# Ranking the experts on chip: 21 places of 64 rows, with down weights in runs of 8 KB

## The reference, cut to what matters

```python
grp = argmax(softmax(h @ w_group + b_group))            # 4 groups
lg = (h @ w_router + b_router)[:, grp]                  # the 8 experts of that group
p_in, e_in = top_k(softmax(lg), 2)                      # two experts of 32 for each token
...
xb = the tokens of each expert, in order of expert, padded
y = (silu(xb @ w_gate[e]) * (xb @ w_up[e])) @ w_down[e] # 1024 -> 512 -> 1024
out = sum of a token's two rows of y, each by its weight
```

## Time and profile before

| | |
|---|---|
| three executions | 2873.58, 2877.64, 2879.01 us, median 2877.64 |
| the profiled execution | 2871.41 us, span of its instructions 2869.6 us |
| granted TensorE clock, mean over the span | 0.993 |
| busy | TensorE (PE) 97%, VectorE (DVE) 39%, ScalarE (ACT) 27%, GpSimd (POOL) 8% |
| HBM | 582.7 MB read, 52.0 MB written, 221 GB/s over the span |
| DMA queue of SyncE | 519.68 MB, 46.9% of 16 engines' span |
| DMA queue of GpSimd | 115.07 MB, 11.7% |

### The profile page before, as it was taken

How to read it: one execution, slowest core, us unless ns; L and a number is a source line. 1 busy time by engine, 2 the same in 40 slices (tenths; PEclk the granted TensorE clock), 3 DMA queues, 4 the chain that set the end, 5 groups by cost and what they waited for, 6 DMA issues and landing times. The chain is left out here.

```text
span 2869.6 us, 64937 instructions
## 1 busy us (share of the span) xinstructions
PE 2778.4 (97%) x27105; PEld 1646.9 (57%) x27109; DVE 1117.6 (39%) x2687; ACT 761.2 (27%) x1601; POOL 234.2 (8%) x396
## 2 busy tenths in 40 slices
PE   7999999999989999999999999989999999999998
PEld 4544655444644467546666666634675566666664
DVE  2582643672643255463222222273443522222224
ACT  1211521102642167421111111153774111111111
POOL 3000011000020000011000000020000100000001
PEclk9999999999999999999999999999999999999999
DMA  7212843123734000347999999872003699999995
GB/s 264 88 59 89 294 122 116 59 74 131 270 108 139 30 2 2 140 176 272 400 400 401 400 400 398 344 255 81 2 2 125 237 383 396 398 398 399 399 399 226
DMA packets 149742, 636.91 MB, mean 222 GB/s; under 512 B 14336, under 2 KB 18528, under 8 KB 133200
## 3 DMA queue, kind: packets, MB, share of 16 engines
q1 hardware_dynamic: 115200, 519.68, 46.9%
q0 software_dynamic: 34384, 115.07, 11.7%
HBM read 582.70 MB, written 52.00 MB: 221 GB/s over the span
## 5 line engine op out<-in xcount | busy, mean ns | idle before, releaser
L1163 PE MATMUL PJ<-WR,XT 128*128 128x512 f32 (+2 forms) x1152 | 477.8, 571 | 6.4 <-ACT XT L140 3.8
L140 ACT ACTIVATE PT<-TR 128x512 f32<-128x512 f32 (+3 forms) x384 | 177.8, 493 | 857.5 <-PE TR L1392 735.4
L1163 PEld LDWEIGHTS PJ<-WR,XT 128*128 128x128 f32 x1152 | 216.6, 192 | 246.2 <-issue 219.0
L140 DVE TENSOR_TENSOR PR<-G 128x384 f32<-128x384 f32 x64 | 35.7, 558 | 738.0 <-ACT G L140 737.5
L1121 PE MATMUL PJ<-WR,XT 128*128 128x512 f32 x576 | 253.2, 595 | 4.1 <-ACT XT L140 2.5
L1372 PE MATMUL SC<-QK,XT 128*64 128x256 f32 x2112 | 242.7, 383 | 0.0
L140 DVE TENSOR_REDUCE SM<-SC 128x1 f32<-128x768 f32 (+6 forms) x208 | 173.6, 835 | 171.9 <-PE SC L1141 167.0
L1323 PE MATMUL PJ<-WR,XT 128*128 128x512 f32 x512 | 225.7, 593 | 1.0 <-issue 1.0
L1372 PE MATMUL SC<-WR,XT 128*64 128x256 f32 x1984 | 226.2, 381 | 0.0
L1372 PEld LDWEIGHTS SC<-QK,XT 128*64 128x64 f32 x2112 | 149.5, 138 | 85.5 <-issue 14.7
L140 ACT ACTIVATE PR<-SC,SM 128x256 f32<-128x256 f32 (+5 forms) x288 | 187.6, 669 | 31.3 <-DVE SM L140 15.0
(11 more groups left out here) (263 smaller groups left out, 3141.1 us busy)
## 6 DMA issues: line engine op xcount, KB each, us to landing
QK<-in_w_gate_dram SPq DMA_DIRECT2D x34, 2048.0 KB, 9.4
WR<-in_w_down_dram SPq DMA_DIRECT2D x34, 2048.0 KB, 15.6
QK<-in_w_up_dram SPq DMA_DIRECT2D x32, 2048.0 KB, 14.3
WR<-in_w_up_dram SPq DMA_DIRECT2D x32, 2048.0 KB, 14.4
WR<-in_w_gate_dram SPq DMA_DIRECT2D x30, 2048.0 KB, 9.4
QK<-in_w_down_dram SPq DMA_DIRECT2D x30, 2048.0 KB, 15.9
WR<-in_w_ada_dram SPq DMA_DIRECT2D x24, 2048.0 KB, 8.5
WR<-in_w_in_dram SPq DMA_DIRECT2D x14, 2048.0 KB, 7.8
```

Of the source, the lines that this page charges most:

```text
L140: return lambda *a, **k: Signal(make(*a, **k), self)
L1163: m = mm(bank[:, 0:n], XT1[:, c, s.t * P:(s.t + 1) * P], w[:, c, 0:n], start=c == 0, stop=c == DC - 1)
```

## The change

The experts are no longer worked on in the order of their numbers. After the counts are known, VectorE ranks them: a key for each expert is 32 times its count plus a term that breaks ties, larger counts come first. The keys of experts 0 to 2 and of 30 and 31 hold no counts, but a constant that keeps them at places 0 to 2 and 30 and 31. The place of an expert (`pos`) is the number of larger keys; the inverse (`ord`) goes to the integer tile `ORD`, which SyncE reads to address the weights. The columns of `IDX` are sorted in the same way into `IDXS` for the gathers.

Places 0 to 8 and the last two keep 96 rows; the 21 places 9 to 29 (`small`) have 64. A small place has no `gate_up_rest` and no 32-row down; its down weights are loaded in two runs of 8 KB for each partition rather than four of 4 KB, so that a partition holds rows 2p and 2p+1 of each half, and `turn_hidden` takes every second column, with two transposes for three; the 64-row down is done in two blocks of 2 x 256 columns instead of one of 2 x 512. Gather, store, silu, hidden product and copies go over 64 rows. The overflow tables are made for 24 blocks rather than 15, with rows past 64 or 96 counted by the expert's place; the guarded loop has groups of six. The loops are cut differently, since a turn of a loop must be alike in all turns: `places` writes out steps up to place 8 and the last ones, and loops over two small places at a time in between. The rows of `YD` that are filled with zeros at the start grow from 16 to 25 blocks of 512 KB.

```diff
 CAP_A, CAP_B = 64, 32
-MAX_OVER = (2 * TOKENS) // (CAP + 1)
-MAIN_SLOTS = EXPERTS * CAP
+FIXED, LARGE = 3, 9
+LAST_TWO = (EXPERTS - 2, EXPERTS - 1)
+
+
+def small(place):
+    return LARGE <= place < LAST_TWO[0]
+
+
+def rows_of(place):
+    return CAP_A if small(place) else CAP
+
+
+def row_base(place):
+    return sum(rows_of(p) for p in range(place))
+
+
+OVER_GROUP = 6
+MAX_OVER = -(-(2 * TOKENS // (CAP_A + 1)) // OVER_GROUP) * OVER_GROUP
+MAIN_SLOTS = row_base(EXPERTS)
 SLOTS = MAIN_SLOTS + MAX_OVER * P
 BLOCKS = EXPERTS + MAX_OVER
 NEAR = (2, 4)
-LAST_TWO = (EXPERTS - 2, EXPERTS - 1)
-OVER_GROUP = 3
+PLACE_KEY = 2.0 ** 17
...
-            most = 2 * (SEQ if l == DEPTH - 1 else TOKENS) // (CAP + 1)
+            most = 2 * (SEQ if l == DEPTH - 1 else TOKENS) // (CAP_A + 1)
             return -(-most // OVER_GROUP)
...
+        turns = (LAST_TWO[0] - 3 - LARGE) // 2
+        evenly = range(LARGE, LARGE + 2 * turns)
+
+        def places(eng, first, end, go):
+
+            for r in range(first, evenly.start):
+                go(lambda a, b: b, r)
+            with eng.Fori(0, turns) as i:
+                for r in evenly[0:2]:
+                    go(lambda a, b: i * a + b, r)
+            for r in range(evenly.stop, end):
+                go(lambda a, b: b, r)
...
-            def load_expert(u, e):
+            def load_expert(u, e, near_rows=False):
                 tile = slot_tile(u.slot)
                 name = {"gate": "w_gate_2", "up": "w_up_2", "down": "w_down_2"}[u.kind]
                 src = ins[name][u.l, bass.ds(e, 1), :, :].rearrange("e k n -> (e k) n")
-                if u.kind == "down":
+                if u.kind == "down" and near_rows:
+                    sp.dma_start(tile.rearrange("p (h x) -> p h x", h=2), src.rearrange("(h p c) n -> p h (c n)", h=2, c=2)).then_inc(
+                        w_loaded[u.slot], 16)
...
-                with sp.Fori(0, 14) as i:
+                sp.wait_ge(order_ready, l + 1)
+
+                def two_experts(i, r):
+                    expert = {p: sp.value_load(ORD[0:1, bass.ds(i * 2 + (r + p - 2), 1)], min_val=0, max_val=EXPERTS - 1)
+                              for p in (2, 3, 4)}
                     for k in range(8, 14):
-                        sp.wait_ge(pj_full if m[k].kind == "down" else sc_full,
-                                   i * (4 if m[k].kind == "down" else 2) + m[k - 6].done)
-                        load_expert(m[k], i * 2 + m[k].e)
+                        down = m[k].kind == "down"
+                        sp.wait_ge(pj_full if down else sc_full, i * (4 if down else 2) + (m[k - 6].done + (r - 2) * (2 if down else 1)))
+                        load_expert(m[k], expert[m[k].e], small(m[k].e + r - 2))
+
+                with sp.Fori(0, 3) as i:
+                    two_experts(i, 2)
+                two_experts(0, 8)
+                with sp.Fori(0, 10) as i:
+                    two_experts(i, 10)
...
-                                    mm(bank[CAP_A * h:CAP_A * (h + 1), k * 512:k * 512 + 256], XET[par][:, c, 0:CAP_A],
-                                       w[:, c, 256 * h:256 * (h + 1)], start=c == 0, stop=c == DC - 1)
+                                    x = mm(bank[CAP_A * h:CAP_A * (h + 1), k * 512:k * 512 + 256], XET[par][:, c, 0:CAP_A],
+                                           w[:, c, 256 * h:256 * (h + 1)], start=c == 0, stop=c == DC - 1)
+                        if small(r):
+                            x.then_inc(sc_full, 1)
...
-                        for k in range(3):
-                            x = turn(TR[:, use % 2, k * P:(k + 1) * P], HID[r % 2][:, k * P:(k + 1) * P], identF)
+                        for k in range(2 if small(r) else 3):
+                            own = slice(k, 2 * P, 2) if small(r) else slice(k * P, (k + 1) * P)
+                            x = turn(TR[:, use % 2, k * P:(k + 1) * P], HID[r % 2][:, own], identF)
...
+                        for k in range(2 if small(r) else 0):
+                            use = J0 + 2 * r + k
+                            pe.wait_ge(pj_free, at_(4, use - 1))
+                            for c in range(4):
+                                o = (c % 2) * P + (c // 2) * CAP_A
+                                for h in range(2):
+                                    x = mm(PJ[CAP_A * h:CAP_A * (h + 1), use % 2, 0:256], HTD[r % 2][:, o:o + CAP_A],
+                                           w[:, c, h * 512 + k * 256:h * 512 + (k + 1) * 256], start=c == 0, stop=c == 3)
+                            x.then_inc(pj_full, 1)
+                        if small(r):
+                            return
...
-                            gate_up_rest(at_, r + 1)
+                            if not small(r + 1):
+                                gate_up_rest(at_, r + 1)
...
-                    with pe.Fori(0, EXPERTS // 2 - 1) as i:
-                        for r in (1, 2):
-                            step(lambda a, b: i * a + b, r)
+                    places(pe, 1, EXPERTS - 1, step)
...
+                    key, pos, cap, rb, la = (R[k] for k in ("key", "pos", "cap", "rb", "la"))
+                    now(STT(key, R["cn"], float(EXPERTS), D32T, ALU.mult, ALU.add))
+                    TS(key[:, 0:FIXED], D32T[:, 0:FIXED], PLACE_KEY, None, ALU.add)
+                    now(TS(key[:, LAST_TWO[0]:], D32T[:, LAST_TWO[0]:], -PLACE_KEY, None, ALU.add))
+                    now(TT(PERM, down(key), across(key), ALU.is_gt))
+                    now(tensor_reduce(pos, PERM, AX.X, ALU.add))
+                    now(TT(PERM, down(pos), across(IOTA[:, 0:EXPERTS]), ALU.is_equal))
+                    now(TT(PERM2, PERM, down(IOTA[:, 0:EXPERTS]), ALU.mult))
+                    now(tensor_reduce(R["ord"], PERM2, AX.X, ALU.add))
+                    tensor_copy(ORD, R["ord"]).then_inc(order_ready, 1)
+                    now(TT(PERM2[0:CAP], PERM[0:CAP], down(R["ix"], CAP), ALU.mult))
+                    now(tensor_reduce(R["ord"][0:CAP], PERM2[0:CAP], AX.X, ALU.add))
+                    tensor_copy(IDXS[0:CAP], R["ord"][0:CAP]).then_inc(idx_sorted, 1)
+
+                    extra = float(CAP - CAP_A)
+                    TS(cap, pos, float(LARGE), extra, ALU.is_lt, ALU.mult)
+                    TS(rb, pos, float(LARGE), extra, ALU.min, ALU.mult)
+                    now(TS(la, pos, float(LAST_TWO[0]), extra, ALU.is_ge, ALU.mult))
+                    now(STT(cap, cap, float(CAP_A), la, ALU.add, ALU.add))
+                    now(TS(la, pos, -float(LAST_TWO[0]), 0.0, ALU.add, ALU.max))
+                    now(STT(rb, pos, float(CAP_A), rb, ALU.mult, ALU.add))
+                    now(STT(rb, la, extra, rb, ALU.mult, ALU.add))
+                    now(TT(la, R["cn"], cap, ALU.subtract))
+                    now(TS(R["nb"], la, 0.0, None, ALU.is_gt))
...
+                    of = [a.rearrange("p (j n) -> p j n", n=EXPERTS) for a in (
+                        R["ov"][:, 0:64 * T], R["ov"][:, 384:384 + 64 * T], TMP[:, 0:64 * T])]
+                    for a, b in zip(of, (R["ob"], rb, cap)):
+                        x = TT(a, own, b.unsqueeze(1).to_broadcast([P, j2, EXPERTS]), ALU.mult)
+                    now(x)
+                    for a, b in zip(of, (o, m, cp)):
+                        x = tensor_reduce(b, a, AX.X, ALU.add)
+                    now(x)
+                    TT(o, o, m, ALU.subtract)
...
-                    def gather(at_, r, e):
-
-                        par = r % 2
+                    def gather(at_, r, ix):
+
+                        par, n = r % 2, rows_of(r)
                         if r >= 2:
                             pool.wait_ge(tr_full, at_(6, T0 + (3 * (r - 2) if r > 2 else 1) + 1))
-                        nc.gpsimd.tensor_copy(XI[0:CAP, par:par + 1], IDX[0:CAP, e]).then_inc(pool_done, 1)
+                        nc.gpsimd.tensor_copy(XI[0:n, par:par + 1], ix[0:n]).then_inc(pool_done, 1)
                         pool.wait_ge(pool_done, at_(2, gathers0 + r + 1))
                         pool.sem_inc(gather_started, 1)
-                        pool.indirect_dma_start(XE[par][0:CAP], None, HDR[:, :],
-                                                bass.IndirectOffsetOnAxis(ap=XI[0:CAP, par:par + 1], axis=0)
+                        pool.indirect_dma_start(XE[par][0:n], None, HDR[:, :],
+                                                bass.IndirectOffsetOnAxis(ap=XI[0:n, par:par + 1], axis=0)
                                                 ).then_inc(xe_loaded[par], 16)
 
-                    def store(at_, r, dst):
+                    def store(at_, r):
                         pool.wait_ge(pj_free, at_(4, J0 + 2 * r + 2))
-                        dma(dst, YR[r % 2][0:CAP]).then_inc(y_stored[r % 2], 16)
+                        n = rows_of(r)
+                        dma(YD[bass.ds(at_(2 * n, row_base(r)), n), :], YR[r % 2][0:n]).then_inc(y_stored[r % 2], 16)
...
+                    pool.wait_ge(idx_sorted, s.l + 1)
```

(71 more changed lines are left out.)

95 lines of the change are left out of this document (50 added, 45 removed).

## The result

The changed kernel took 2852.02 us (median of 4 executions, 2849.17 to 2855.89) against 2878.32 for the kernel before (4 executions): a ratio of 0.991, 95% interval 0.9889 to 0.993. It is faster by 26 us; forecast were 58, with a range that ended at 2848. The profiled execution took 2850.72 us with a span of 2849.0.

A forecast was written before the change was run, and what follows sets the result against it. TensorE and the DMA queue were taken as limits within 1% of each other, the queue setting small steps. Gain 42.2 from steps plus 22.2 from early weights, less 6.0 routing: 58.4, so 2819.2 us; range 2786 to 2848.

The forecast's parts named there:

- with a third fewer gathered rows 0.2 of it goes: Small step's queue: the stretch at 317 GB/s while down meets the gather costs 0.7 us; 0.2 us of that is saved.
- rival C: Expert stages: gather falls beside 16 KB runs, the sag to 317 GB/s goes, 1.6 to 1.9 us a step; 2783 to 2796; chance 0.08.
- B: Expert stages: only bytes count, the tail takes half of the stock; 2848 us, sign a spacing over 17.1; chance 0.13.
- the stock: Weights landed early before each layer's last up half: 12.4 and 9.8 us gained whole, 22.2 in all.
- Before the last up load 20.5 small steps count: Expert stages: 20.5 steps per layer each save 1.0 us of queue time, 21 us per layer (12 to 39).
- Routing: Ranking on VectorE adds 14.2 and 13.8 us; TensorE waits 2.9 and 1.9; loss 6.0 us with the clock.
- Unrolled steps: TensorE's 12 unrolled steps of 31 lie beside other work, so they cost nothing.
- 8 KB runs: Small places' down weights in 8 KB runs instead of 4 KB: 0.1 us saved a step.
- rival D: Expert stages: TensorE, cut by waits, loses its clock; at 1.2 GHz throughout 24.0 us a step, 3140 us; chance 0.05.
- E: Small places: an expert with over 64 rows makes overflow blocks run, 87 us in a layer, 2906 us; chance 0.02.
- F: Expert stages: TensorE's saving comes in full, as if DMA had room, 239 less 6: 2645 us; chance 0.02.
- A: Expert stages, the forecast: the queue sets 16.7 us a step; 2819 us, bounds 2796 to 2840; chance 0.70.

The follow-up runs named there:

- halves: Changed kernel, with each of the 64 token rows of a small place gathered as two 2 KB halves into all 128 partitions: 2808.14 us, ratio 0.9753.
- spread: Changed kernel, small places' gather replaced by a plain load of 64 token rows into every second of 128 partitions (output not the reference's): 2806.84 us, ratio 0.9757.
- ranked_only: Changed kernel without small places: experts ranked, steps written out, but 96 rows and down in 4 KB runs in all 32 places: 2905.91 us, ratio 1.0097.
- ranked_rolled: Changed kernel, ranked, 96 rows in all 32 places, loops from place 3 instead of 9, so two steps written out in front, not eight: 2882.74 us, ratio 1.003.
- other_source: Changed kernel, small places' gather replaced by a plain load of 64 4 KB rows of gate weights into the lower 64 partitions: 2853.98 us, ratio 0.9921.
- direct: Changed kernel, small places' indirect gather replaced by a plain DMA of the 64 first token rows, same bytes and destination: 2853.6 us, ratio 0.9922.
- pad_rows: Changed kernel, with unfilled rows p of an expert given index p instead of 0, so the gather doesn't reread token row 0: 2854.68 us, ratio 0.9917.

## Why the prediction was wrong

- **The bound** was read right: the queue sets the small step, TensorE waits, the share is 1.01. TensorE's step is 12.2, forecast 12.0: turning every second column takes 0.50 us for two transposes, where 0.37 would be two thirds of the earlier trace rows. The 64-row down takes 3.67, as said.
- **The step that failed** is "with a third fewer gathered rows 0.2 of it goes". I took the sag of the earlier trace rows as something that shrinks with the rows. It grew from 3.3 to 4.1 us, and what the weights' packets lose in it from 0.7 to 1.0 us a step, with a third fewer rows. That is measured; why a gathered row got dearer is open (see Sizes). So the small step is 17.2 us instead of 16.7, and it would have been 16.0 without the sag: rival C's number for the step, but by a remedy of its own, not by what C named. C said the sag goes when the gather falls beside 16 KB runs; in the changed kernel two thirds of the loss is in such packets, and it doesn't go. B's mark (a spacing over 17.1) came true, its half of the stock didn't.
- **"Before the last up load 20.5 small steps count"** was mis-sized: 17 got shorter. That places 9 to 11 stand behind loads and gathers of large places, and the last ones beside the 96-row gathers of 30 and 31, is argued, not tried. With `halves`, 3.5 steps of 1.7 us in two layers are 12 of the 16 us by which the forecast's own sum (2878 - 70 - 22 + 6 = 2792) would have missed. The queue gave 7 us where 42 were forecast: 7 of the difference are the 3.5 steps, 19 the size of the gain per step (0.37 and 0.55 us instead of 1.03), 9 what was lost ahead of place 12 and behind 29. In layer 0 `spread` lost 0.5 us ahead and nothing behind (table of landings), so most of that comes with the gathers into adjacent partitions too.
- **The stock** of 22.2 us was gained whole, as said; 7.9 us were lost again elsewhere, 3 a layer had been named.
- **Routing**: VectorE's price came as forecast: from the end of the routing before it to the operation that releases L1493 it took 14.0 and 13.3 us more, forecast 14.2 and 13.8. The waits were only 0.48 and 0.31 us, forecast 2.9 and 1.9, since in this execution VectorE began that stretch 2.2 and 1.1 us earlier, measured against TensorE. In layer 0 that is luck: it began at 1294.87 us, and with the same code in `spread`, `halves` and `ranked_only` at 1296.5 to 1297.8. `ranked_only` had a wait of 2.27 at the same place. All that comes with ranking, in loops, costs 8 us (5 to 12) by `ranked_rolled`; 6 were forecast.
- **Unrolled steps** were costed at nothing because they "lie beside other work". They do, but not beside free DMA: 19 us by `ranked_only` and `ranked_rolled`. In `halves` the price can't be told from nothing; in the changed kernel it wasn't measured.
- **8 KB runs**: 0.25 us a step, forecast 0.1. **The clock** (rival D) did fall to 1.2 GHz in part of the steps (0.89 above, down in 5.36 us instead of 3.67), in steps in which TensorE waited for weights. The slower kernel that D described didn't come: the queue stayed busy throughout (1.01), and TensorE waited less. That it cost nothing isn't shown: `other_source` had 1.00 and 405 GB/s in the same window, but over its whole span the same 0.975, and over stretches of 60 us this kernel, `direct`, `pad_rows` and `other_source` ran at 392 to 408 GB/s with a clock of 1.00 and at 389 to 399 with 0.91 or less. E and F didn't come.
- **The range of A** doesn't follow from its own terms: 39 us a layer give 2878 - 78 - 22 + 6 = 2784, not 2796, which is just outside the stated range too.

The Trainium skill (SBUF — State Buffer, Door 1: The DMA port swizzle) says that a transfer into partitions 0 to 63 reaches only 8 of 16 ports, for which its figure is about 218 GB/s. The trace agrees: 215. I had not weighed it, and it speaks against this change. By the Trainium skill (DMA: Bandwidth & Descriptors, Back-pressure in remote DMA), for transfers between cores, writes that stall at a full port also stall the DMA engine's other queues; the slowed packets of the weights above agree with that for a local load. Of instruction fetch the Trainium skill (Runtime: NRT & Kernel Launch, Instruction fetch mechanics) says that crossing into the next block is mostly hidden; the 19 us of `ranked_only` speak against it where DMA is the bound, as far as they come from the fetches.

## What to carry to other kernels

Before costing a smaller transfer by its bytes, look at which partitions it writes: here 64 adjacent partitions made each gathered byte 2.7 times as dear as spread ones. Don't scale a disturbance with the bytes of what causes it: with a third fewer rows it grew. When a queue has no slack, find everything else that uses its engines, code fetches too, and ask what happens once it falls behind. When the bound moves, count the steps for which it has really moved by landing times, not by the number of steps changed.

## What I had not expected of the hardware

A gather of 64 rows of 4 KB alone runs at 215 GB/s into 64 adjacent partitions, and while it runs every packet of another queue takes 1.2 to 1.5 times as long (16 KB up to about 900 ns instead of 615, 8 KB 480 instead of 312), though that queue writes all 128 partitions. As 128 halves, or in every second partition, it slows nothing. Stores out of 64 partitions slow nothing either. And steps written out instead of looped, with 0.33 instead of 0.13 MB of code fetched at the start of layer 0's experts, were enough to start a delay of 19 us.
